# Three norm steps of the mixers, each moved one planner step later, and the first w_out block moved with them

## The reference, cut to what matters

```
ssd:    y = (y_diag + y_off + X*d) * silu(z);   group_rms_norm(y, norm_g, 2 groups of 512)
mlstm:  h = num / max(|den|, exp(-m));  h = h * sigmoid(o_pre);  group_rms_norm(h, norm_g, 4 heads of 128)
rwkv7:  y = scan over time, normed per head, gated
x = x + concat([y_ssd, y_mlstm, y_rwkv]) @ w_out
```

## Time and profile before

| what | value |
|---|---|
| median of the runs | 1797.14 us |
| profiled execution: time, span | 1798.5 us, 1796.5 us |
| TensorE busy | 1725.7 us, 96% |
| VectorE, ScalarE, GpSimd busy | 70%, 50%, 21% |
| mean granted TensorE clock | 0.984 |

### The profile page before, as it was taken

One profiled execution on the slowest core, in us unless ns is written; L12 is line 12 of the kernel. 1 busy time (PEld: TensorE's weight loads), 2 busy tenths in 40 slices (PEclk: granted clock), 3 DMA queues, 4 the chain that ended last, 5 costly groups with the idle time before them and its releaser, 6 DMA issues.

```text
span 1796.5 us, 35508 instructions
## 1 busy us (share of the span) xinstructions
PE 1725.7 (96%) x15248; PEld 1611.8 (90%) x15248; DVE 1256.6 (70%) x2101; ACT 889.7 (50%) x1566; POOL 369.0 (21%) x316
## 2 busy tenths in 40 slices
PE   7999999999899999999999999989999999979997
PEld 6999988887799998999998888779999888879987
DVE  5876675856667776677676576566787665789974
ACT  5664435323445654566443533344565555556652
POOL 3552000000212651156200000021265200121110
PEclk9999999999899999999999999989999999989999
DMA  8655522211146565565552221114556552335442
GB/s 301 238 222 194 213 94 94 75 46 49 49 162 258 214 233 185 212 252 211 194 215 92 94 95 34 40 48 166 222 210 234 188 192 104 118 141 181 174 151 104
DMA packets 44492, 282.86 MB, mean 157 GB/s; under 512 B 6064, under 2 KB 6704, under 8 KB 17712
## 3 DMA queue, kind: packets, MB, share of 16 engines
q1 hardware_dynamic: 44336, 280.60, 42.7%
HBM read 279.53 MB, written 1.05 MB: 156 GB/s over the span
## 4 chain that ended last, share of the span: by engine, by line
PE 83%; DVE 11%; ACT 3%; issue 1%; DMA 1%; POOL 0%; SPq 0%; DVEq 0%; ACTq 0%
PE bank L489 16%; PE bank L491 15%; PE bank L490 15%; PE bank L497 10%; PE bank L985 8%; PE bank L498 5%; PE bank L1581 4%; DVE WL L480 2%; ACT WH L475 2%; PE bank L1848 1%; PE bank L1125 1%; DVE XC L1054 1%; DMA ring<-wst 1%; PE bank L527 1%; PE bank L1858 0%
## 5 line engine op out<-in xcount | busy, mean ns | idle before, releaser
L489 PE MATMUL bank<-XNH,WH 128*128 128x256 f32 (+1 forms) x2176 | 620.7, 285 | 17.9 <-DVE XNL L573 12.3
L480 DVE TENSOR_TENSOR WL<-ring,WH 128x2048 fp32r<-128x2048 f32 (+1 forms) x235 | 509.4, 2170 | 162.9 <-ACT WH L475 162.7
L491 PE MATMUL bank<-XNH,WL 128*128 128x256 f32 (+1 forms) x2176 | 616.6, 283 | 0.0
L490 PE MATMUL bank<-XNL,WH 128*128 128x256 f32 (+1 forms) x2176 | 614.5, 282 | 0.0
L475 ACT ACTIVATE WH<-ring 128x2048 fp32r<-128x2048 f32 (+1 forms) x235 | 405.5, 1729 | 211.4 <-PE bank L491 133.1
L489 PEld LDWEIGHTS bank<-XNH,WH 128*128 128x128 f32 x2176 | 412.9, 190 | 23.6 <-DVE XNL L573 12.3
L490 PEld LDWEIGHTS bank<-XNL,WH 128*128 128x128 f32 x2176 | 414.3, 190 | 0.0
L491 PEld LDWEIGHTS bank<-XNH,WL 128*128 128x128 f32 x2176 | 414.1, 190 | 0.0
L497 PE MATMUL bank<-HP,WH 128*128 128x512 f32 x770 | 267.6, 392 | 0.8 <-POOL HP L882 0.7
L498 PE MATMUL bank<-HP,WL 128*128 128x256 f32 x770 | 215.5, 280 | 0.0
L985 PE MATMUL bank<-XN,ring 128*128 128x256 f32 x832 | 200.1, 389 | 0.0
(11 more groups left out here) (476 smaller groups left out, 2612.4 us busy)
## 6 DMA issues: line engine op xcount, KB each, us to landing
ring<-wst SPq DMA_DIRECT2D x206, 1024.0 KB, 4.8
ring<-wst SPq DMA_DIRECT2D x80, 704.0 KB, 4.2
LP<-lp SPq DMA_DIRECT2D x1, 1872.0 KB, 7.1
LP<-lp SPq DMA_DIRECT2D x1, 1792.0 KB, 8.4
X<-xin SPq DMA_DIRECT2D x2, 512.0 KB, 4.7
out<-X SPq DMA_DIRECT2D x4, 256.0 KB, 2.5
C<-cst SPq DMA_DIRECT2D x1, 193.0 KB, 10.7
AL<-cst SPq DMA_DIRECT2D x1, 192.0 KB, 10.6
```

The source lines that it names most:

```text
L480: e.do.tensor_tensor(WL[:, slot[q], 0:n], ring[:, i % NSLOT, 0:n], WH[:, slot[q], 0:n].bitcast(F32), ALU.subtract).then_inc(*w_dve.up("low ...
L489: e.do.matmul(o, WH[:, s, cols], xh, start=first, stop=False)
L490: e.do.matmul(o, WH[:, s, cols], xl, start=False, stop=False)
L491: return e.do.matmul(o, WL[:, s, cols], xh, start=False, stop=last)
```

## The change

The `yield`s of both ends are moved. SSD: on ACT the two squares stand in steps of their own, `ssd:25` and `ssd:26`, where both stood in `ssd:24`; on POOL their sums stand in `ssd:26` and `ssd:27`; the gate stays in `ssd:24`; PE's sums, DVE's root, the rows, the scaling and the low parts are each one step later (28, 29, 31, 31 to 34, 35). mLSTM: the output gate stands in `scan:43`, a step of its own behind the last head, and all that follows it is one step later on every engine. `ahead:0` may come only when `ssd` has done 28 steps (before: 24).

```diff
@@ order_of
-                return done["ssd"] >= 24 and done["scan"] >= 42 and done["proj"] == steps["proj"]
+                return done["ssd"] >= 28 and done["scan"] >= 42 and done["proj"] == steps["proj"]
@@ pe_scan, ahead of the sums; act_scan, ahead of the square
+            yield
@@ pool_scan
-            for _ in range(49):
+            for _ in range(50):
@@ pe_ssd, ahead of the sums
-            for _ in range(3):
+            for _ in range(4):
@@ act_ssd
             for g in range(2):
+                yield
                 e.wait_ge(*d_dve.on("gated", l, g))
                 e.do.activation((xd, xe)[g]..., Y[:, 4 * g:4 * g + 4, :], ACT.Square)
-            for _ in range(6):
+            for _ in range(5):
@@ dve_ssd, behind the gate
-            for _ in range(4):
+            for _ in range(5):
@@ pool_ssd
             for g in range(2):
+                yield
                 q = (xd, xe)[g]
...
-            for _ in range(9):
+            for _ in range(8):
```

## The result

The changed kernel takes 1807.73 us (1807.19 to 1808.12, 4 runs), beside 1798.18 of the kernel before (4 runs): ratio 1.005, 95% interval 1.0038 to 1.0062. It is slower by half a per cent; forecast was 1799.9 with a range of 1793 to 1804, so the time lies outside it. The direction was right (+2.8 forecast for both layers), the size was off by a factor of more than three (+9.5).

The account below looks back on a forecast made before the run. PE is busy 96% of the span, so only its idle stretches can be won. The terms, with -0.7 for the gate inside, came to +1.4 us a layer, +2.8 for both: 1797.14 becomes 1799.9, range 1793 to 1804.

Parts of the forecast that it names:

- Output gate in its own step: mLSTM's end: SSD's mix and PE's L1848 come 1.4 us earlier, the rows' wait falls to 1.8; -0.7 us a layer remains.
- PE comes at 451.5 and waits 0.7: At SSD's last m4, no longer covered by mLSTM's sums: PE waits 0.7 us for DVE's last product, ending at 452.2.
- 1.2 more with the clock at 2.4 GHz: Bound on the output gate's gain: about 1.2 us more if the rows and mix run at the high clock.
- mLSTM's root one step later: DVE's root, 460.75 to 462.85, behind Y copies 0 and 1: PE's R steps of lanes 2 and 3 wait about 1.3 us.
- paid by what goes: The root's 1.3 us wait is offset because the rows that stood at 461.68 (1.16 us) come two steps later.
- SSD's gate and squares: Gate runs 466.0 to 468.4, lane 3's copy precedes ACT's squares, and PE's 5.69 us stall at the lane is gone.
- What is late next: PE's stall moves to POOL's squares; DVE's low part meets POOL, root from 479.5, rows end 483.7, 1.4 us later a layer.
- Nothing behind them changes in number, so the 1.4 stays: Behind SSD's rows the last steps keep their order, so the 1.4 us delay a layer persists unchanged.
- The slower one: Rival: the low clock slides past 489 into `w_out`'s dense part; +13 us for both layers, 1810; chance 0.06.
- The sum: Both layers together: +1.4 us a layer, +2.8 in all, median 1799.9 us.

Follow-up runs that it names:

- m2_s: Kernel before with mLSTM's output gate alone moved to `scan:43`, plus the SSD part and `ahead:0` as in the change: 1790.25 us, ratio 0.9958.
- after_f12: Changed kernel with unread products on PE ahead of its waits for DVE's mix, the last m4, GpSimd's squares and SSD's rows: 1800.94 us, ratio 1.0007.
- m2_s_r: Changed kernel with mLSTM's square and sums left where they were, root and rows one step later: 1798.93 us, ratio 0.9997 to the kernel before.
- after_a29: Changed kernel with `ahead:0` moved directly behind `ssd:29`: 1804.77 us, ratio 1.0025 to the kernel before.
- m2_only: Kernel before with mLSTM's output gate alone moved to `scan:43`; square, sums and root where they were: 1793.8 us, ratio 0.9975.
- m_only: Kernel before with only mLSTM's part of the change; SSD and `ahead:0` as before: 1803.27 us, ratio 1.0024.
- M: mLSTM's part of the change: output gate in `scan:43`, everything behind it one step later; alone on the kernel before, ratio 1.0024.
- S: The SSD part of the change; alone on the kernel before, with `ahead:0` behind `ssd:27`, ratio 0.9992.
- ms24: mLSTM's and SSD's parts of the change, but `ahead:0` as early as in the kernel before: 1808.64 us, ratio 1.0052.
- s_only: Kernel before with only SSD's part of the change and `ahead:0` behind `ssd:27`; mLSTM as before: 1797.75 us, ratio 0.9992.
- a_only: Kernel before with only `ahead:0` moved behind `ssd:27`; both ends of the mixers in their old steps: 1797.41 us, ratio 0.9994.
- before_f2: Kernel before with unread products ahead of PE's waits for last rows, lane stall, squares and SSD's rows, none at the last m4: 1793.66 us, ratio 0.9975.
- after_f1: Changed kernel with 3 unread products ahead of PE's wait for DVE's mix and 4 ahead of the last m4's: 1803.86 us, ratio 1.0028.

## Why the prediction was wrong, step by step

- *Output gate in its own step*, the wait of the rows: right. Forecast 1.8, measured 1.58 (3.17 before).
- The same step, "PE comes at 451.5 and waits 0.7": the wait was 2.02. I had carried over durations of the low clock (2.07 for the rows, 2.59 for the half tile behind them) into a stretch which then ran at 1.00 (1.16 and 1.89), so PE was there at 450.0 and not at 451.5, with nothing to do until 452.0. The bound "1.2 more with the clock at 2.4 GHz" looked at the rows alone: I counted the gain of the clock, and did not see that PE then waits for DVE. The half tile behind the rows, in the kernel before:

```profile
450.02 2.59 PE L985 MATMUL bank<-XN,ring 128*128 128x256 f32 x8
```

- Still the same step: the wait itself ended when forecast (452.0, forecast 452.2). What put the stamps off was the clock behind it. The forecast had 1.95 us for the sums and 2.23 for the next half tile; they took 3.57 and 3.15 at the low clock. The forecast for the end of that half tile was 459.3 (459.97 less 0.7), measured 460.81: 1.5 us late, and the steps behind it kept 0.9 to 1.6 us of that up to the end of SSD's rows. A low piece on the rows, ahead of this wait, would have been covered by it; behind it nothing covers it. The prediction looked for the low clock behind the wait at the rows, and put none behind the wait that it had itself found at the m4.
- The same step, the whole of it (-0.7 a layer): the term that failed most. In m2_s, with the gate moved and the sums where they were, the half tile ends at 455.36, before at 459.97: the gate alone is worth 4.6 us a layer there, by the wait and by the low pieces that go. The sums' move costs 5.2, more than all of it. after_f12, from its last rows (446.48) to the end of its half tile (457.41), needs 10.9 us, m2_s_r 8.9 and the changed kernel 14.1: so 2.0 for PE's wait that nothing covers, and 3.2 because the clock fell directly behind that wait, onto the sums (3.57 for 1.95) and the half tile (3.15 for 1.99). I wrote that the sums "covered a wait", and priced only the wait.
- *mLSTM's root one step later*, forecast as a wait of 1.3 us "paid by what goes": the wait was right (1.26 at 464.79), but it is not paid. The runs give it 7 us for both layers (m2_s_r against m2_s, 3.0 a layer in the rows). At 453.79 the root stood where DVE had time for it; a step later it is queued behind L1060, which waits for ACT's copy of tile 39's half (6.65 us of idle time in the changed kernel, at 461.54), and two lanes' copies. The root began at 462.37, forecast was 460.75. The prediction's own stamps had the first rows end at 465.1, where they ended at 462.84 before: it saw the delay and didn't price it as one.
- *SSD's gate and squares*: right in kind. The stall at the lane goes (0.45 left of 5.69). The gate came at 467.62 for 466.0, the squares of GpSimd at 472.40 for 470.95, by what the two steps ahead had lost.
- *What is late next*: right and well sized. L1873 waits 5.3 (4 to 6 forecast), L480 at 475.04 for 474.65 and 2.82 us long (2.3 to 3.4), GpSimd done at 478.44 for 477.5, SSD's root at 480.67 (479.5), the rows end at 484.93 (483.7). The mutual lengthening of DVE and GpSimd (2.82 and 2.65) was taken from the earlier trace rows and came out so; after_a29, in which they don't meet, gains 0.0025, of which the meeting is a part.
- *"Nothing behind them changes in number, so the 1.4 stays"*: wrong. The rows ended 2.7 us later than before and DVE's first addition to X behind `w_out` came 3.7 later (512.00 for 508.32): behind the rows the clock was still low, and eleven groups of lane products from 484.86 on took 0.42 to 0.48 instead of 0.28 to 0.33. The window 481 to 488 has 0.55 for 0.92.
- *Rivals.* The slower one (the low stretch slides into later work, chance 0.06) was right in kind only: the low stretch slid onto the lanes' last steps (up to 487.3), and did not reach the place that I named (488 to 502 ran at 1.00). I had taken the clock as something that moves only with the large stall; in fact it also fell behind a new wait of 2 us.
- *The sum.* By the runs, for both layers: gate alone -4.5 (m2_only), the SSD part on it -3.0 (m2_s), root a step later +7.0, sums a step later +9.5, together +9.0. The prediction had -2.8 for the gate, +1.4 for the sums (its wait of 0.7), and what is left, +4.2, for root and SSD part together; the runs have +4.0 for these two. So the term that carried the miss is the sums' move, 1.4 forecast and 9.5 measured; the gate's gain was too small by 1.7. These prices hold in this order and with the SSD part in: without it, root and sums together cost 0.0049 (8.8 us, m_only against m2_only), with it 0.0092 (16.5).

What stays open: why M and S lose more together (1.005) than apart (1.0024 and 0.9992). ms24 excludes the place of `ahead:0`. The traces of m_only and ms24 differ in one place that fits. ACT's squares, in m_only and in ms24:

```profile
471.73 2.19 ACT L1914 ACTIVATE XE<-Y 128x1024 f32<-128x1024 f32 x2 [0.72 <-DVE Y L1977]
```

```profile
477.52 1.99 ACT L1915 ACTIVATE XE<-Y 128x1024 f32<-128x1024 f32 x2
```

In m_only they stand in `ssd:24`, ahead of the rounding of mLSTM's second pair of tiles, which M moved to `scan:49`. In ms24 they stand in `ssd:25` and `ssd:26`, behind it. From the last rows on they start 25.2 us later in m_only and 29.1 in ms24, and SSD's root 31.6 and 35.3; of these 3.9 and 3.7 us, 1.6 were there at DVE's gate already (23.9 and 25.5). No run changed this alone, so it is argued and not shown. A low piece on dense work between 1450 and 1480 is in the traces of the changed kernel, s_only, a_only, ms24, m2_s_r, after_a29 and before_f2, and not in those of before, m_only, m2_only, m2_s and after_f12; each takes about 1.7 us (0.001), and why it comes was not tried. The differences above are not cleared of it.

## What to carry to other kernels

When a step is moved away, ask of each engine what its instructions stood in front of: a product that fills a wait is worth the wait and the clock behind it. Take the durations of a stretch at the clock that it will have after the change, also for the engine that must arrive in time, and then look again who waits. Change one instruction's place at a time: here the output gate alone, in its step, gains 0.25% (m2_only), and the move of what follows it loses all of that and more (m_only).

## What was not expected of the hardware

- Products without a reader, ahead of a wait, made the kernel faster: 4.0 us for seven in each layer (after_f1), 7.7 us for all (after_f12), and 4.5 us for the kernel before. PE's busy time rises, the sums fall from 3.57 to 1.95 us.
- The first low stretch of the changed kernel (6.8 us at 0.50) came behind waits of 1.58 and 2.02 us, each shorter than the 3.17 which had stood there, and is as long as the two low pieces before (3.4 and 3.3 us); m2_s, with the first of these waits alone, had 1.00 up to 467.
- DVE's products of one tensor with a scalar for each partition (L1721) took 1.40 us for two at 477.78, while GpSimd ended its narrow add and began mLSTM's low parts, and 0.57 for three at 464.84, where GpSimd stood still. So in this kernel not only DVE's operations with two tensors were slow beside GpSimd.
